# A streaming encoder trunk on one core: reordering the weight and adaLN transfers of the down projections, and writing y in eight transfers

## The chip, the cores and the metric

The kernel runs on one NeuronCore of a Trainium2 chip. The metric is the time of one execution on the device in microseconds (us), the median of several runs. The profile is one further execution, taken by the hardware profiler.

## The reference, cut to what matters

Two layers run over 544 tokens (512 of a prompt, 32 of a running stream), 1024 features wide. Each layer is a half-step SwiGLU FFN, a mixer (latent attention and retention heads), and a second half-step FFN. Each of the three is normalised before and after, and shifted, scaled and gated by vectors that come from a conditioning vector c.

```python
mods = (jax.nn.silu(c) @ ada_w[l] + ada_b[l]).reshape(c.shape[0], 3 * N_SUB, D_MODEL)
h = modulated_pre(x, norm_pre[l, 0], mods, 0)
x = gated_post(x, swiglu(h, ffn_w1[l, 0], ffn_w3[l, 0], ffn_w2[l, 0]), norm_post[l, 0], mods, 0, 0.5)
...
def swiglu(h, w1, w3, w2):
    return (jax.nn.silu(h @ w1) * (h @ w3)) @ w2
```

The last product of `swiglu`, with `w2` (2816 x 1024), is the down projection. There are four in the program: two FFNs in each of two layers. Beside it, the kernel computes the `mods` of the sub-layers that follow.

## The kernel before

All work is written by hand for each engine, with semaphores between them; the order of an engine's instructions is the order in the code. Activations are held feature-major: 128 partitions, eight feature tiles, 544 tokens.

**The chain of a weight chunk.** Every weight is float32 and is multiplied as a sum of a high and a low part. SyncE (SP) loads a chunk into one of two slots of `raw` (`load_chunk`, L356); ScalarE (ACT) rounds it to `w_hi` (`high` L968, `high_at` L975); GpSimd (POOL) subtracts, giving `w_lo` (`low`, L458); TensorE (PE) multiplies (`tile3`, L545 to L549). Each has two slots. SP loads chunk n once the low part of chunk n-2 is made (`lo_done`). ACT rounds chunk n once PE has finished chunk n-2 (`w_used`) and the chunk has landed.

**A down projection.** It has 16 chunks of 704 KB (11 weight tiles of 128x128 each), two for each of the eight output tiles. They are called c0 to c15 here; PE's work on one is 66 matmuls. ACT's order in it is: round c2 and c3, square and scale output tile 0; round c4 and c5, square and scale output tile 1; and so on. The scaling (L1068) needs `mul_post`, a column of `mods`, so the first of them waits for VectorE (DVE) to make it (`post_columns`, L1316).

**The ada tiles.** `ada_w` comes in tiles of 128x1024 (512 KB), in a ring of four slots (`ADA_RING`). DVE multiplies each with the two conditioning rows and sums (`ada_group`, L1292, two operations for each tile), four tiles to a group; after a group two additions put the result into `mods` (L1300). The first FFN of a layer (s = 0) does 48 tiles during its down projection, the second (s = 1) 24. `mul_post` is ready after the first two groups. SP may load tile t once tile t-4 is consumed (`ada_done`). The ring lies over `h_hi`, the input of the up projection, so its first four loads wait until PE has used the last chunk of the up projection.

**Order on SP.** Weight chunks and ada tiles go through the same instruction stream on SP, so a load stands behind the waits of all loads ahead of it. In `down`, each chunk load is followed by a share of tiles: none, four, four and four in the first four chunks at s = 0, later three after each chunk; at s = 1 none, four, two, two, later two after each, and none in the last four.

**The end of a down projection.** Before PE may sum the squares by token (`token_sums`, L562), it waits for all ada tiles of the phase (`ada_done`), since these sums use the PSUM banks where the conditioning rows lie. Then follow the root on ACT (L982), the reciprocal (L1326) and, for each feature tile m, `wide_v` (L1333) and the addition to `x` (L1337 on DVE, L484 on POOL for m = 1, 3, 5).

**The end of the program.** SP waits for all eight tiles of `x`, sends y out in one transfer (L444), and waits for it.

Of the kernel before, what the change touches and what calls it, by code (L numbers as in the profile page):

```python
# [24 lines left out]
P = 128  # L25
D = 1024
DEPTH = 2
# [7 lines left out]
KD = D // P  # L35
# [11 lines left out]
DN_T = FT // 2  # L47
UP_C = 2 * FT
DN_C = 2 * KD
# [11 lines left out]
MODS = 9 * KD  # L61
ADA_RING = 4
# [34 lines left out]
def streaming_trunk(nc, a, o):  # L97
    ctx = ExitStack()
    with ctx:
        def sb(name, shape, dt=F32):  # L100
            return ctx.enter_context(nc.sbuf_tensor(name, shape, dt))
# [22 lines left out]
        def signal(name, per_layer, before=0):  # L124
            return Signal(ctx.enter_context(nc.semaphore(name)), per_layer, before)


        x = sb("x", [P, KD, T])
# [118 lines left out]
        w_used = signal("w_used", CH, 2)  # L247

        ada_landed = [signal(f"ada_landed{i}", 16 * MODS // ADA_RING, 16 * 16 // ADA_RING) for i in range(ADA_RING)]
        ada_done = signal("ada_done", 2 * MODS, 2 * 16)  # L250
# [4 lines left out]
        x_new = [signal(f"x_new{i}", 12, 4) for i in range(2)]  # L255
# [78 lines left out]
        y_out = signal("y_out", 0)  # L334
# [12 lines left out]
        @block.sync  # L347
        def _(sp):
            def load_ada(tile, slot):
                sp.dma_start(ada_w[:, slot, :], a["ada"][bass.ds(tile, 1)].rearrange("a p n -> p (a n)"))\  # L350
                    .then_inc(ada_landed[slot].sem, 16)

            def load_chunk(l, c, slot, src, width):

                sp.wait_ge(lo_done.sem, lo_done.at(l, c - 1))
                sp.dma_start(raw[:, slot, 0:width], src.rearrange("a p n -> p (a n)"))\  # L356
                    .then_inc(landed[slot].sem, 16)

            sp.dma_start(c_all[:, :, :], a["c"].partition_broadcast(P)).then_inc(c_in.sem, 16)
            for t in range(ADA_RING):  # L360
                load_ada(t, t)
            sp.dma_start(ada_b[:, :], a["ada_b"]).then_inc(const_first.sem, 16)
            sp.dma_start(g_pre[:, :], a["g_pre"]).then_inc(const_first.sem, 16)
            for t in range(ADA_RING, 12):
                sp.wait_ge(ada_done.sem, 2 * (t - ADA_RING + 1))
                load_ada(t, t % ADA_RING)
            sp.dma_start(x[:, :, :], a["x"]).then_inc(x_in.sem, 16)
            for t in range(12, 16):
                sp.wait_ge(ada_done.sem, 2 * (t - ADA_RING + 1))
                load_ada(t, t % ADA_RING)  # L370
            consts = [(ident, "ident"), (half_ones, "half_ones"), (k_decay, "k_decay"), (k_decays, "k_decays"),
                      (cross, "cross"), (own_head, "own_head"), (state_decay, "state_decay"),
                      (g_post, "g_post"), (g_lat, "g_lat")]
            for t, n in consts:
                sp.dma_start(t[tuple([slice(None)] * len(t.shape))], a[n]).then_inc(const_in.sem, 16)

            def ffn(l, s):
                base = FFN_C[s]
                with sp.Fori(0, UP_C // 2) as i:
                    for k in range(2):  # L380
                        load_chunk(l, base + i * 2 + k, k, a["w_up"][bass.ds((l * 2 + s) * UP_C + i * 2 + k, 1)], KD * P)

                first, per = ((0, ADA_A // 4), (ADA_A, ADA_B // 3))[s]

                def down(i, first_time=False, ada=True):
                    for k in range(4):
                        load_chunk(l, base + UP_C + i * 4 + k, k % 2,
                                   a["w_dn"][bass.ds((l * 2 + s) * DN_C + i * 4 + k, 1)], DN_T * P)
                        if first_time:

                            tiles = (0, 0, ADA_RING, (per + ADA_RING) // 2, per)[k:k + 2]
                        else:
                            tiles = (k * per // 4, (k + 1) * per // 4)
                        for t in range(*tiles) if ada else ():
                            if not first_time or t >= ADA_RING:
                                sp.wait_ge(ada_done.sem, ada_done.at(l, 2 * first + 2 * per * i + 2 * (t - ADA_RING + 1)))
                            elif t == 0:

                                sp.wait_ge(w_used.sem, w_used.at(l, base + UP_C))
                            load_ada(l * MODS + 16 + first + i * per + t, t % ADA_RING)  # L400

                down(0, first_time=True)
                with sp.Fori(1, 4 - s) as i:
                    down(i)
                if s == 1:
                    down(3, ada=False)

            for l in range(DEPTH):
                ffn(l, 0)
                for c in range(MIX_C):  # L410
                    load_chunk(l, MIX_C0 + c, c % 2, a["w_mix"][bass.ds(l * MIX_C + c, 1)], KD * P)
                    if c == 1:

                        sp.wait_ge(w_used.sem, w_used.at(l, MIX_C0))
                        sp.dma_start(rope_tab[:, :, :], a["rope"]).then_inc(tables.sem, 16)
                        sp.dma_start(state_in[:, :, :], a["state"][bass.ds(l, 1)].rearrange("a p i v -> p (a i) v"))\
                            .then_inc(tables.sem, 16)
                    if c == Z_C + 1:

                        sp.wait_ge(w_used.sem, w_used.at(l, MIX_C0 + Z_C))  # L420
                        sp.dma_start(decay[:, :, :], a["decay"]).then_inc(decay_in.sem, 16)
                    if c == OUT_C0 + 1:
                        sp.wait_ge(kv_ready.sem, kv_ready.at(l, 1))
                        sp.dma_start(o["kv"][bass.ds(l, 1)].rearrange("a p n -> p (a n)"), kv[:, :]).then_inc(stored.sem, 16)
                        sp.wait_ge(rope.sem, rope.at(l, 3))
                        sp.dma_start(o["kpe"][bass.ds(l, 1)].rearrange("a p n -> p (a n)"), kpe[0:ROPE, :]).then_inc(stored.sem, 16)
                        sp.wait_ge(st_ev.sem, st_ev.at(l, 16))
                        sp.dma_start(o["state_p"][bass.ds(l, 1)].rearrange("a p i v -> p (a i) v"), state_p[:, :, :])\
                            .then_inc(stored.sem, 16)
                        sp.dma_start(o["state_s"][bass.ds(l, 1)].rearrange("a p i v -> p (a i) v"), state_in[:, :, :])\  # L430
                            .then_inc(stored.sem, 16)

                        sp.wait_ge(ro_mm.sem, ro_mm.at(l, 4))
                        sp.dma_start(cache_kv[:, 0:PAST], a["cache_kv"][bass.ds(l, 1)].rearrange("a p n -> p (a n)"))\
                            .then_inc(caches.sem, 16)
                        sp.dma_start(cache_pe[:, 0:PAST], a["cache_pe"][bass.ds(l, 1)].rearrange("a p n -> p (a n)"))\
                            .then_inc(caches.sem, 16)
                        sp.dma_start(cache_tok[:, :, :], a["cache_tok"][bass.ds(l, 1)].rearrange("a p b r -> p (a b) r"))\
                            .then_inc(caches.sem, 16)
                ffn(l, 1)  # L440

            for new in x_new:
                sp.wait_ge(new.sem, new.at(DEPTH, 0))
            sp.dma_start(o["y"], x[:, :, :]).then_inc(y_out.sem, 16)  # L444
            sp.wait_ge(y_out.sem, 16)
            sp.wait_ge(stored.sem, stored.at(DEPTH, 0))


# [1314 lines left out]
```

## Time and profile before

| | us |
|---|---|
| median of 3 runs | 2562.56 (2561.49 to 2564.19) |
| profiled execution, its own time | 2563.67 |
| its span, first to last instruction | 2561.9 |
| PE busy | 2387.9 (93%) |
| DVE busy | 1295.2 (51%) |
| ACT busy | 809.5 (32%) |
| POOL busy | 892.4 (35%) |
| mean granted TensorE clock | 0.977 of full speed |
| mean DMA rate | 106 GB/s |

The span is what the trace covers; 1.8 us of the execution's own time lie outside it. Busy shares are averages over stages: PE is nearly always busy, so what counts is what lies between its instructions, and what runs at the end when it has finished.

### The profile page before, as it was taken

How to read it: one execution, taken by the hardware profiler on the slowest of the kernel's cores; microseconds unless marked ns; L12 is line 12 of the kernel's file. 1: busy time of each engine (PE TensorE's matmuls, PEld its weight loads, DVE VectorE, ACT ScalarE, POOL GpSimd, SP SyncE). 2: the span in 40 equal slices, each digit the busy share in tenths (PEclk: the TensorE clock that was granted, in tenths of full speed). 3: DMA queues.
4: the chain of work that ended last, by engine and by line, in shares of the span. 5: the costliest groups of instructions: out<-in, count | busy, mean ns of one | idle time of the engine just before them, and what ended most of it. 6: DMA issues, size and time to landing. Idle time of an engine off the chain costs nothing.

```text
span 2561.9 us, 44088 instructions
## 1 busy us (share of the span) xinstructions
PE 2387.9 (93%) x17588; PEld 2247.4 (88%) x17588; DVE 1295.2 (51%) x2006; ACT 809.5 (32%) x1371; POOL 892.4 (35%) x384
## 2 busy tenths in 40 slices
PE   1999999999888999999999999999988899999997
PEld 1999999899456999999989999999964588999996
DVE  7333379774473243337243334986835515333561
ACT  2332222433233432323242223224323334322321
POOL 1334334443000543334443433444420034343343
PEclk9999999999899999999999999999989999999998
DMA  6222268323100222226312223761220011222451
GB/s 223 75 90 82 90 231 287 118 84 112 41 1 1 66 83 85 87 86 238 136 58 90 82 89 137 281 242 60 80 80 33 1 44 64 90 82 90 173 206 59
DMA packets 71509, 272.50 MB, mean 106 GB/s; under 512 B 8641, under 2 KB 10049, under 8 KB 70529
## 3 DMA queue, kind: packets, MB, share of 16 engines
q1 hardware_dynamic: 71424, 271.35, 30.8%
q8 instruction: 56, 0.92, 0.1%
q14 instruction: 29, 0.23, 0.0%
HBM read 267.87 MB, written 3.45 MB: 106 GB/s over the span
## 4 chain that ended last, share of the span: by engine, by line
PE 77%; DVE 11%; issue 6%; ACT 2%; DMA 1%; POOL 1%; DVEq 0%; SPq 0%; POOLq 0%; ACTq 0%
PE ps L545 22%; PE ps L549 22%; PE ps L546 21%; PE ps L859 2%; PE ps L903 2%; PE ps L555 1%; DVE ret_q L1443 1%; PE ps L855 1%; DVE ret_k L1443 1%; PE ps L593 1%; DVE wide_v L1333 1%; DVE wide_v L1292 1%; PE ps L769 1%; DVE x L1337 1%; DVE h_lo L1352 1%
## 5 line engine op out<-in xcount | busy, mean ns | idle before, releaser
L458 POOL TENSOR_TENSOR w_lo<-raw,w_hi 128x1024 fp32r<-128x1024 f32 (+1 forms) x304 | 789.6, 2597 | 1604.1 <-ACT w_hi L975 1295.8
L545 PE MATMUL ps<-h_hi,w_hi 128*128 128x274 f32 x3296 | 897.8, 290 | 4.8 <-DVE z_tmp L1412 4.8
L546 PE MATMUL ps<-h_lo,w_hi 128*128 128x274 f32 x3296 | 898.7, 290 | 0.0
L549 PE MATMUL ps<-h_hi,w_lo 128*128 128x274 f32 x3296 | 690.4, 291 | 0.0
L545 PEld LDWEIGHTS ps<-h_hi,w_hi 128*128 128x128 f32 x3296 | 626.5, 190 | 6.3 <-issue 6.2
L546 PEld LDWEIGHTS ps<-h_lo,w_hi 128*128 128x128 f32 x3296 | 620.8, 188 | 0.2
L975 ACT CAST w_hi<-raw 128x1024 fp32r<-128x1024 f32 (+1 forms) x236 | 268.3, 1137 | 876.1 <-PE ps L549 736.6
L549 PEld LDWEIGHTS ps<-h_hi,w_lo 128*128 128x128 f32 x3296 | 521.1, 188 | 0.0
L545 PE MATMUL ps<-u_hi,w_hi 128*128 128x272 f32 x1408 | 380.7, 289 | 13.1 <-POOL w_lo L458 13.1
L546 PE MATMUL ps<-u_lo,w_hi 128*128 128x272 f32 x1408 | 381.0, 289 | 0.0
L1292 DVE CUSTOM_DVE_ANT_0 wide_v<-ada_w,ps 128x1024 bf16<-128x1024 f32 x288 | 332.0, 1216 | 47.4 <-DMA ada_w<-in_ada 29.1
L1370 DVE TENSOR_TENSOR wide_v<-ps,wide_rinv 128x548 f32<-128x548 f32 x88 | 64.1, 729 | 451.6 <-PE ps L549 451.6
L549 PE MATMUL ps<-u_hi,w_lo 128*128 128x272 f32 x1408 | 291.0, 288 | 0.0
L545 PEld LDWEIGHTS ps<-u_hi,w_hi 128*128 128x128 f32 x1408 | 266.3, 189 | 14.9 <-POOL w_lo L458 14.9
L546 PEld LDWEIGHTS ps<-u_lo,w_hi 128*128 128x128 f32 x1408 | 265.7, 189 | 0.0
L1375 DVE SCALAR_TENSOR_TENSOR wide_v<-wide_v,wide_s 128x512 f32<-128x512 f32 (+1 forms) x176 | 194.5, 1143 | 110.2 <-ACT wide_s L1031 110.2
L549 PEld LDWEIGHTS ps<-u_hi,w_lo 128*128 128x128 f32 x1408 | 222.8, 189 | 0.0
L583 PE MATMUL ps<-h_hi,w_hi 128*128 128x274 f32 x192 | 64.5, 356 | 68.4 <-ACT h_hi L998 59.9
L968 ACT CAST w_hi<-raw 128x1024 fp32r<-128x1024 f32 x68 | 71.1, 1046 | 170.7 <-PE ps L549 113.6
L1034 ACT CAST u_hi<-wide_v 128x544 f32 (+1 forms) x88 | 56.9, 647 | 214.3 <-DVE wide_v L1375 214.3
L1326 DVE RECIPROCAL tok_inv<-tok_root 128x5 f32<-128x5 f32 x6 | 1.1, 190 | 218.0 <-ACT tok_root L982 218.0
L583 PEld LDWEIGHTS ps<-h_hi,w_hi 128*128 128x128 f32 x192 | 46.0, 239 | 72.7 <-issue 59.9
(228 smaller groups left out, 2565.7 us busy)
## 6 DMA issues: line engine op xcount, KB each, us to landing
raw<-in_w_up SPq DMA_DIRECT2D x176, 512.0 KB, 3.2
ada_w<-in_ada SPq DMA_DIRECT2D x160, 512.0 KB, 4.5
raw<-in_w_dn SPq DMA_DIRECT2D x64, 704.0 KB, 4.9
raw<-in_w_mix SPq DMA_DIRECT2D x64, 512.0 KB, 3.3
decay<-in_decay SPq DMA_DIRECT2D x2, 2048.0 KB, 8.2
x<-in_x SPq DMA_DIRECT2D x1, 2176.0 KB, 8.9
rope_tab<-in_rope SPq DMA_DIRECT2D x2, 1088.0 KB, 4.9
out_y<-x SPq DMA_DIRECT2D x1, 2176.0 KB, 7.3
```

The lines of the kernel that those rows point to most:

```text
L458: pool.tensor_tensor(w_lo[:, slot, 0:width], raw[:, slot, 0:width], w_hi[:, slot, 0:width].bitcast(F32), ALU.subtract).then_inc(lo_done.se ...
L545: pe.matmul(ps[:, bank + t, 0:half], wh, hi[:, n], start=start, stop=False)
L546: pe.matmul(ps[:, bank + t, 0:half], wh, lo[:, n], start=False, stop=False)
L549: last = pe.matmul(ps[:, bank + t, 0:half], wl, hi[:, n], start=False, stop=stop)
L583: pe.matmul(ps[:, 2 * w + t, 0:HW], w_hi[:, w, k * P:(k + 1) * P], h_hi[:, k, n], start=k == 0, stop=False)
L859: pe.matmul(ps[:, j, 0:w], q_pe[:, h // 4, q], own_keys[h % 4][:, 0:w], start=False, stop=True)\
L968: nc.scalar.copy(w_hi[:, slot, 0:width], raw[:, slot, 0:width]).then_inc(hi_done.sem, 1)
L975: nc.scalar.copy(w_hi[:, k, 0:width], raw[:, k, 0:width]).then_inc(hi_done.sem, 1)
L1034: nc.scalar.copy(u_hi[:, bass.ds(i * 2 + f, 1), :].rearrange("p a n -> p (a n)"), tmp_v[:, f, :]).then_inc(up_hi.sem, 1)
L1292: v_.tensor_tensor_reduce(junk[v], ada_w[:, t, :], c_row, 1.0, 0.0, ALU.mult, ALU.add, acc[:, v, t:t + 1]).then_inc(ada_done.sem, 1)
L1370: v_.tensor_tensor(halves(wide_v[:, f, :]), wide_pair(4 * f + 2), halves(wide_rinv[:, :]), ALU.mult)\
L1375: v_.scalar_tensor_tensor(out=wide_v[:, f, at], in0=wide_v[:, f, at], scalar=wide_v[:, f, T + 2 * v:T + 2 * v + 1], in1=wide_s[:, f, at], ...
```

## The change

In both FFNs, the loads of c2 and c3 now follow right behind the first four ada tiles, and the next ada tiles come after them. At s = 0 every later share of tiles stands three tiles further back (`ahead = 3`): the load of c4 is preceded by tiles up to 8 where it was 11, and the last three tiles of the phase follow after the last share. At s = 1 only the place of c3 changes. At the end, y goes out in eight transfers of 272 KB, each as soon as its tile of `x` is ready.

```diff
                 first, per = ((0, ADA_A // 4), (ADA_A, ADA_B // 3))[s]
-
-                def down(i, first_time=False, ada=True):
+                ahead = 3 if s == 0 else 0
+
+                def load_dn(i, k):
+                    load_chunk(l, base + UP_C + i * 4 + k, k % 2,
+                               a["w_dn"][bass.ds((l * 2 + s) * DN_C + i * 4 + k, 1)], DN_T * P)
+
+                def ada_tile(i, t):
+
+                    sp.wait_ge(ada_done.sem, ada_done.at(l, 2 * first + 2 * per * i + 2 * (t - ADA_RING + 1)))
+                    load_ada(l * MODS + 16 + first + i * per + t, t % ADA_RING)
+
+                def down(i, ada=True):
                     for k in range(4):
-                        load_chunk(l, base + UP_C + i * 4 + k, k % 2,
-                                   a["w_dn"][bass.ds((l * 2 + s) * DN_C + i * 4 + k, 1)], DN_T * P)
-                        if first_time:
-
-                            tiles = (0, 0, ADA_RING, (per + ADA_RING) // 2, per)[k:k + 2]
-                        else:
-                            tiles = (k * per // 4, (k + 1) * per // 4)
-                        for t in range(*tiles) if ada else ():
-                            if not first_time or t >= ADA_RING:
-                                sp.wait_ge(ada_done.sem, ada_done.at(l, 2 * first + 2 * per * i + 2 * (t - ADA_RING + 1)))
-                            elif t == 0:
-
-                                sp.wait_ge(w_used.sem, w_used.at(l, base + UP_C))
-                            load_ada(l * MODS + 16 + first + i * per + t, t % ADA_RING)
-
-                down(0, first_time=True)
+                        load_dn(i, k)
+                        for t in range(k * per // 4, (k + 1) * per // 4) if ada else ():
+                            ada_tile(i, t - ahead)
+
+                load_dn(0, 0)
+                load_dn(0, 1)
+                sp.wait_ge(w_used.sem, w_used.at(l, base + UP_C))
+                for t in range(ADA_RING):
+                    load_ada(l * MODS + 16 + first + t, t)
+                load_dn(0, 2)
+                load_dn(0, 3)
+                for t in range(ADA_RING, per - ahead):
+                    ada_tile(0, t)
                 with sp.Fori(1, 4 - s) as i:
                     down(i)
                 if s == 1:
                     down(3, ada=False)
+                for t in range(per - ahead, per) if s == 0 else ():
+                    ada_tile(3, t)
...
-            for new in x_new:
-                sp.wait_ge(new.sem, new.at(DEPTH, 0))
-            sp.dma_start(o["y"], x[:, :, :]).then_inc(y_out.sem, 16)
-            sp.wait_ge(y_out.sem, 16)
+            for m in range(KD):
+                sp.wait_ge(x_new[m % 2].sem, x_new[m % 2].at(DEPTH - 1, 2 * (KD // 2) + m // 2 + 1))
+                sp.dma_start(o["y"][:, m, :], x[:, m, :]).then_inc(y_out.sem, 16)
+            sp.wait_ge(y_out.sem, 16 * KD)
```

## Rows read from the trace of the kernel before

**Rows 1.** The page: shares of the chain that ended last, by engine.
```profile
PE 77%; DVE 11%; issue 6%; ACT 2%; DMA 1%; POOL 1%; DVEq 0%; SPq 0%; POOLq 0%; ACTq 0%
```
**Rows 2.** Waits of PE in down projections 1, 2, 3: total us, times, longest.
```profile
PE ps L545 <- POOL w_lo L458: 5.6, 4, 3.2
...
PE ps L545 <- POOL w_lo L458: 1.1, 1, 1.1
...
PE ps L545 <- POOL w_lo L458: 5.5, 2, 3.2
```
**Rows 3.** Timeline of SP, down projection 1: start, duration, engine, line, transfer, count.
```profile
334.28 0.49 SPq L356 DMA_DIRECT2D raw<-in_w_dn  x1
343.00 7.18 SPq L350 DMA_DIRECT2D ada_w<-in_ada  x4
350.23 0.43 SPq L356 DMA_DIRECT2D raw<-in_w_dn  x1
...
361.29 0.34 SPq L356 DMA_DIRECT2D raw<-in_w_dn  x1
```
**Rows 4.** Timeline of ACT, down projection 1; in brackets idle time before and its releaser.
```profile
332.49 1.37 ACT L975 CAST w_hi<-raw 128x1408 fp32r<-128x1408 f32 x1 [4.77 <-PE ps L549]
...
355.74 1.37 ACT L975 CAST w_hi<-raw 128x1408 fp32r<-128x1408 f32 x1 [11.10 <-DMA raw<-in_w_dn]
...
361.50 0.84 ACT L1068 ACTIVATE o_ffn<-ps,mul_post 128x272 f32<-128x272 f32 x2 [3.87 <-DVE mul_post L1316]
```
**Rows 5.** Timeline of POOL, down projection 1: the low part of c3.
```profile
357.19 3.17 POOL L458 TENSOR_TENSOR w_lo<-raw,w_hi 128x1408 fp32r<-128x1408 f32 x1 [9.25 <-ACT w_hi L975]
```
**Rows 6.** Windows of one chunk: us, busy PE, PEld, DVE, ACT, POOL, clock, DMA share, GB/s.
```profile
357.10:365.40 8.30, 5.14 (x29) 4.99 (x28) 7.61 (x19) 1.55 (x5) 3.17 (x1) 0.79 0.82 272
...
1193.30:1201.60 8.30, 7.19 (x57) 7.08 (x57) 7.28 (x15) 2.80 (x5) 5.72 (x3) 1.00 0.71 259
```
**Rows 7.** Timeline of ACT, down projections 2 (two rows) and 3 (the last).
```profile
1160.38 1.37 ACT L975 CAST w_hi<-raw 128x1408 fp32r<-128x1408 f32 x1 [4.76 <-PE ps L549]
...
1188.91 0.84 ACT L1068 ACTIVATE o_ffn<-ps,mul_post 128x272 f32<-128x272 f32 x2 [8.33 <-DVE mul_post L1316]
...
1580.08 1.37 ACT L975 CAST w_hi<-raw 128x1408 fp32r<-128x1408 f32 x1 [4.76 <-PE ps L549]
```
**Rows 8.** Timeline of PE: first token sums, ending down projections 1, 2 and 3.
```profile
472.73 1.17 PE L562 MATMUL ps<-ones,squares 128*128 128x1 f32 x10
...
1293.85 1.17 PE L562 MATMUL ps<-ones,squares 128*128 128x1 f32 x10
...
1719.69 1.17 PE L562 MATMUL ps<-ones,squares 128*128 128x1 f32 x10
```
**Rows 9.** Timeline of DVE: a pause, and the last ada tiles of projections 1 and 3.
```profile
433.79 2.56 DVE L1300 TENSOR_TENSOR mods<-acc,ada_b 128x4 f32 x2 [0.16 <-DVE acc L1292]
...
466.19 0.08 DVE L1292 DVE_READ_ACCUMULATOR2_ANT acc<- 128x1 f32 x1
...
1714.11 0.08 DVE L1292 DVE_READ_ACCUMULATOR2_ANT acc<- 128x1 f32 x1
```
**Rows 10.** DMA issues: transfer, count, KB each, median us from issue to landing.
```profile
ada_w<-in_ada SPq DMA_DIRECT2D x160, 512.0 KB, 4.5
raw<-in_w_dn SPq DMA_DIRECT2D x64, 704.0 KB, 4.9
...
out_y<-x SPq DMA_DIRECT2D x1, 2176.0 KB, 7.3
...
out_kv<-kv SPq DMA_DIRECT2D x2, 272.0 KB, 4.1
...
out_state_p<-state_p SPq DMA_DIRECT2D x2, 128.0 KB, 1.9
```
**Rows 11.** Windows inside the y transfer and before it; columns as in group 6.
```profile
2544.00:2554.00 10.00, 0.00 (x0) 0.00 (x0) 9.83 (x13) 0.00 (x0) 4.00 (x3) 0.55 0.00 0
...
2556.00:2558.00 2.00, 0.00 (x0) 0.00 (x0) 0.00 (x0) 0.00 (x0) 0.00 (x0) 0.50 1.00 418
```

## The prediction, made before the changed kernel was run

> **What bounds the kernel now.** I read the page first. The chain that ended last is PE for 77% [rows 1], so a change in the transfers can only gain where PE stands still, or after PE's last instruction. The waits of PE, asked for each down projection, show where it stands still: 5.6 us in four waits in the first, 1.1 us in the second, 5.5 us in the third [rows 2]; the fourth repeats the second (1.0 us). The releaser is the low part of a weight chunk, made by POOL, so the chain of that chunk is followed back.
>
> In projection 1, SP issues the load of c2 at 334.28, then four ada tiles from 343.00 to 350.2, and only then c3 at 350.23 [rows 3]. The tiles wait for DVE to free their slots, and c3 stands behind them in SP's stream although its own slot is long free. ACT is idle 11.1 us for it and rounds at 355.74 [rows 4]; POOL makes the low part from 357.19 to 360.4 [rows 5]; PE stands still for 3.2 us [rows 2]. The same happens to c4, behind four more tiles, at 361.29 [rows 3]. The windows show a second price: after the long wait the granted clock is 0.79 of full speed over a chunk's time, while after the 1.1 us wait of projection 2 it is 1.00 [rows 6]. So the 3.2 us wait is followed by a stretch at the lower level (1.2 GHz), and the short one is not.
>
> The whole price is best read from the length of a projection, from the rounding of c1 (released when PE begins) to the first token sums [rows 4, 7, 8]:
>
> - projection 1: 472.73 - 332.49 = 140.24 us
> - projection 2: 1293.85 - 1160.38 = 133.47 us
> - projection 3: 1719.69 - 1580.08 = 139.61 us
>
> All have the same 16 chunks. Those with 48 ada tiles lose 6.8 and 6.1 us against those with 24.
>
> **Part 1: c2 and c3 ahead of tiles 4 and on.** At s = 0, c3 can go out behind c2 once its slot is free, some 10 us sooner than 350.23, and lands long before PE asks for it. The 3.2 us wait and the slow clock behind it go. c4 now follows tile 8 instead of tile 11. DVE consumes a tile in about 2.3 us (the four issues spanning 7.18 us are three such steps plus the first issue [rows 3]), so c4 goes out about 3 x 2.4 = 7 us sooner, near 354, and lands by the median of 4.9 us [rows 10] near 359.
>
> Then something else is late: ACT. Before c4 it scales output tile 0, which needs `mul_post`. That comes at 361.50 - 332.49 = 29.0 us after the start in projection 1 and 28.5 us in projection 2 [rows 4, 7]. It depends only on DVE's eight tiles, which the change leaves alone. In projection 2 exactly this leaves PE 1.1 us short at c4 [rows 2]. So I take for projections 1 and 3 the length of 2 plus the 0.5 us by which `mul_post` comes later: 133.47 + 0.5 = 133.95 us.
>
> **Part 2: the next bound, DVE.** PE may not start its token sums before all 48 tiles are done. DVE's last one ends at 466.27 - 332.49 = 133.8 us in projection 1 and 1714.19 - 1580.08 = 134.1 us in projection 3 [rows 4, 7, 9]. Before, 6.4 and 5.5 us of slack hid this. Now it comes level with PE: 133.95 against 133.85, and 133.95 against 134.15 (each with 0.05 for the semaphore). The later of the two counts:
>
> - projection 1: 140.24 - 133.95 = 6.3 us gained
> - projection 3: 139.61 - 134.15 = 5.5 us gained
>
> Does the shift by three tiles make DVE later? A tile may be loaded when the tile four before it is done, and is wanted three tiles on, 3 x 2.3 + 1.1 (the additions between groups) = 8 us later; it lands in 4.5 us by the median [rows 10]. What could hold it is the chunk load now ahead of it, which waits for the low part of chunk n-2. For c5 that is some 6 us earlier than the slot of its next tile comes free, and some distance stays up to c15: PE's 12 chunks of 8.3 us, 1.6 for the c4 wait and 4.7 for rounding and low part of c13 give 106 us, while the slot of its next tile (42) comes free after 39 tiles, at about 108 us by the pace of DVE. So SP still waits for DVE and not for POOL; the shift costs nothing. If this cover went, each us would be paid in full, since DVE has no slack left. The other way, c16 (the first mixer chunk) now stands behind tiles up to 47 and lands about 128 us after the start; PE wants it only after the turn-over, over 10 us later.
>
> At s = 1 only c3 moves. PE did not wait for it, only for `mul_post` at c4, which stays: 0 us. The two clock stretches are in the lengths and are not counted again. The mixer's loads shift with the rest, since the same order on SP follows.
>
> **Part 3: y.** One transfer of 2176 KB lands 7.3 us after its issue [rows 10], at 418 GB/s in the middle [rows 11]. The eight tiles of `x` are made one after another in the 10 us before it, with DVE busy and no DMA [rows 11]. A piece of 272 KB takes 0.67 us at that rate, so seven are gone or nearly so when the last tile is ready, and SP needs under 0.5 us for each issue [rows 3]. Only the last piece counts. It is bounded by a write of 128 KB, 1.9 us, and one of 272 KB, 4.1 us, which shared the DMA engines with loads [rows 10]. Worked out from the big one: 7.3 less 5.3 us of moving is 2.0, plus 0.67, gives 2.6; I take 2.5. Gain 7.3 - 2.5 = 4.8 us (3.2 to 5.4).
>
> **The sum.** 6.3 + 5.5 + 4.8 = 16.6 us. The profiled execution's own time is 2563.67, its span 2561.9, so it stands 1.1 us above the median of the runs, 2562.56. From its own time the sum gives 2547.1; from the median, by which the result is judged, 2546.0. I predict 2546.0.
>
> A rule of the Trainium skill speaks against part 3. On the page "DMA: Bandwidth & Descriptors", section "Anatomy of one DMA", a transfer costs a fixed 2.0 us and its bytes at 436 GB/s. By that an estimate for the large one is 7.1 us, which the 7.3 us row bears out, and 2.6 us for a piece; the section "Bandwidth" advises transfers of 1 MiB or more.
>
> **The rivals.**
>
> *The eight pieces are not in flight together.* If each had to wait for the one before, they would take 8 x 2.6 = 21 us from about 2545, when the first tile is ready [rows 11], and end at 2566 instead of 2561.5: part 3 costs 4.5 us instead of giving 4.8, and the time is 2555.3. The advice of the named page on small transfers would bite in this case. Against it: SP issues three ada tiles 2.3 us apart, each landing in 4.5 us [rows 3, 10], so transfers overlap. Chance 3%.
>
> *DVE becomes the bound by more than a hair.* At three places in projection 1 the additions to `mods` took longer than their usual 0.3 us, up to 2.6 us [rows 9]. With no slack, one more of these in each projection costs 2 x 2.3 = 4.6 us: 2550.6. Chance 18%.
>
> *The c4 wait drops the clock.* If it grows from 1.6 to over 2 us in both, PE gets a slow stretch there, some 2 us each (140.24 - 133.47 less 5.6 - 1.1 of waits leaves 2.3 for the slow clock): 2550.4. Chance 10%.
>
> *The stall moves on.* c5 or c6 come late instead, by half of what is gained now (5.9 us): 2551.9. For it: the DMA share is already 0.82 there [rows 6]. Against: both go out over 3 us before they are wanted. Chance 7%.
>
> *DVE is starved* (the slower side). The chunk ahead of each three tiles holds them beyond the 8 us of cover. There are 13 such places in each of two projections; the sum is eaten when each costs 16.6 / 26 = 0.64 us, and at 1.3 us each the time is 2563 + 17 = 2580. This needs tiles landing in over 9 us against 4.5 [rows 10]. Chance 4%.
>
> **How the numbers follow.** Likeliest case, as summed: 58%, with 2543.5 to 2549 as its own range (y at its bounds, `mul_post` half a us either way, pauses on DVE smaller or larger). A measurement here tells 0.2%, about 5 us, from no change; so faster means below 2557.4, and all cases but starvation lie there; part of unforeseen ones may not. Faster 0.91, same 0.05, slower 0.04. The range of 8 in 10 takes in the DVE, clock and moved-stall cases: 2543.0 to 2552.5.
>
> **What would show it.** Right: c3 issued before 341 in projection 1; no wait of PE over 2 us in any down projection, one of 1 to 2 us at c4 in each; clock 1.00 in the chunk behind it; lengths of projections 1 and 3 near 134 us, 2 and 4 unchanged; the last ada tile and the token sums within 0.5 us of each other; last y piece landing 2 to 3 us after its issue. Wrong: idle DVE before L1292 with a DMA as releaser in projections 1 and 3; token sums released by DVE more than 1 us late; PE waits at c5 or later.

## The result and the profile after

The changed kernel takes 2556.37 us (median of 12 runs, 2551.33 to 2560.58), the kernel before, measured beside it, 2562.30 us (12 runs, 2559.77 to 2564.32). The ratio is 0.9976 with an interval of 0.9968 to 0.9985: 0.24% faster, a little more than the 0.2% that a measurement can tell from no change. The forecast was 2546.0 us with a range from 2543.0 to 2552.5, so 5.9 us came of 16.6, and the time lies above the range. The span of the profiled execution is 2555.6 us, 6.3 us less than the one before.

I look first at what the change was to do directly. The timeline of SP in down projection 1, after:

```profile
334.15 3.23 SPq L356 DMA_DIRECT2D raw<-in_w_dn  x2
342.88 11.10 SPq L350 DMA_DIRECT2D ada_w<-in_ada  x5
354.31 1.09 SPq L356 DMA_DIRECT2D raw<-in_w_dn  x1
```

Both c2 and c3 are out by 337.4, and c4 goes out at 354.31, 7.0 us sooner than in [rows 3]. And the DMA issues of the page:

```profile
out_y<-x SPq DMA_DIRECT2D x8, 272.0 KB, 2.1
```

A piece of y lands 2.1 us after its issue, against 7.3 for the whole [rows 10]. So the orders went where they were meant to go. Now the waits of PE in down projection 1, 2 and 3 (us in all, times, longest), after:

```profile
PE ps L571 <- DVE acc L1301: 1.8, 1, 1.8
...
PE ps L554 <- POOL w_lo L467: 1.6, 1, 1.6
...
PE ps L554 <- POOL w_lo L467: 1.1, 1, 1.1
...
PE ps L554 <- POOL w_lo L467: 4.1, 1, 4.1
...
PE ps L571 <- DVE acc L1301: 1.8, 1, 1.8
```

The 3.2 us waits for c3 [rows 2] are gone. What is new is a wait for DVE (`acc`, the ada tiles) at the end of projections 1 and 3, 1.8 us each, and a wait of 4.1 us at c4 in projection 3, where projection 1 has 1.6. Both end at work that DVE has not done yet.

Lengths, from the rounding of c1 (332.36 and 1576.03 in the ACT timeline after) to the first token sums:

| projection | before | forecast | after |
|---|---|---|---|
| 1 | 140.24 | 133.95 | 468.26 - 332.36 = 135.90 |
| 2 | 133.47 | 133.47 | 133.47 |
| 3 | 139.61 | 134.15 | 1717.20 - 1576.03 = 141.17 |
| 4 | 133.39 | 133.39 | 133.39 |

Projection 1 gained 4.3 us of 6.3. Projection 3 became 1.6 us longer where 5.5 us were to be gained. The timeline of PE at the two ends, after:

```profile
468.26 1.55 PE L571 MATMUL ps<-ones,squares 128*128 128x1 f32 x10 [1.80 <-DVE acc L1301]
469.67 2.27 PE L571 MATMUL ps<-ones,wide_s 128*128 128x1 f32 x10
...
476.42 0.60 PE L592 MATMUL ps<-h_hi,w_hi 128*128 128x274 f32 x1 [2.54 <-ACT h_hi L1007]
...
1717.20 1.25 PE L571 MATMUL ps<-ones,squares 128*128 128x1 f32 x10 [1.82 <-DVE acc L1301]
...
1725.06 0.59 PE L592 MATMUL ps<-h_hi,w_hi 128*128 128x274 f32 x1 [2.54 <-ACT h_hi L1007]
```

From the token sums to the first matmul of the mixer it takes 8.16 and 7.86 us. Before, it took 6.23 us behind projection 1 (from 472.73 [rows 8]) and 6.76 us behind projection 3 (from 1719.69 to 1726.45):

```profile
473.76 1.25 PE L562 MATMUL ps<-ones,wide_s 128*128 128x1 f32 x10
...
478.96 0.60 PE L583 MATMUL ps<-h_hi,w_hi 128*128 128x274 f32 x1 [2.54 <-ACT h_hi L998]
```

That is another 1.9 and 1.1 us lost.

The account of the two traces, span against span: 0.1 gained before projection 1; +4.3 in it; -1.9 in its turn-over; +1.6 in the mixer of the first layer; 0 in projection 2; -1.6 in projection 3; -1.1 in its turn-over; +0.1 up to projection 4; +4.8 from there to the end, where y is. Together 6.3 us. The 1.6 us of the mixer can't be put down to the change: in the trace of the kernel that has only the y part (below), whose loads are as before, the mixers of the two layers take 393.3 and 395.3 us from their first matmul to their token sums, where the trace of the kernel before has 395.2 and 393.5.

**Where DVE lost the time.** Its work is the same, 2006 instructions on both pages, but it is busy for 1307.6 us instead of 1295.2. Of the 12.4 us more, 8.3 are longer additions to `mods` in projections 1 and 3, and 4.1 are two operations behind them (`mul_pre`, below). Timeline of DVE in projection 3, after (the bracket gives idle time and its releaser):

```profile
1592.52 1.22 DVE L1301 CUSTOM_DVE_ANT_0 wide_v<-ada_w,ps 128x1024 bf16<-128x1024 f32 x1
...
1593.94 3.32 DVE L1309 TENSOR_TENSOR mods<-acc,ada_b 128x4 f32 x2 [0.20 <-DVE acc L1301]
1597.55 1.22 DVE L1301 CUSTOM_DVE_ANT_0 wide_v<-ada_w,ps 128x1024 bf16<-128x1024 f32 x1 [0.29 <-DVE mods L1309]
```

Two additions on 128x4 take 3.32 us. Elsewhere the same pair takes 0.28 or 0.29. Nothing stands in brackets that would explain it: a wait inside an instruction counts as its busy time. So I looked at what the other engines did in these 3.3 us, and found POOL:

```profile
1594.02 3.22 POOL L467 TENSOR_TENSOR w_lo<-raw,w_hi 128x1408 fp32r<-128x1408 f32 x1 [3.31 <-ACT w_hi L984]
```

POOL's subtraction ends at 1597.24 and the addition at 1597.26. In the kernel before, the pause of 433.79 [rows 9] meets POOL in the same way:

```profile
433.03 3.22 POOL L458 TENSOR_TENSOR w_lo<-raw,w_hi 128x1408 fp32r<-128x1408 f32 x1 [3.71 <-ACT w_hi L975]
```

It starts in the middle of that subtraction and ends with it, at 436.3. In all kernels of this study each addition over 0.4 us ends at most 0.03 us from the end of an instruction of POOL. Mostly that is a subtraction of weights; for the rest, which take at most 1.4 us, it is an operation on the squares (128x544, about 1.35 us). (The Trainium skill says so on the page "SBUF — State Buffer", section "SBUF: two separate sides": an operation of VectorE with two inputs in SBUF and one of GpSimd that reads SBUF take one port pair in turns, each for its whole instruction. The trace agrees: 0.15 us became up to 3.2.)

A pair costs 0.3 us or up to 3.3, by where it meets POOL. Counting what the additions took over their usual 0.16 us, from their rows in the timelines: projection 1 went from 5.4 to 6.5 us, projection 3 from 4.9 to 12.2 us, with four pauses of about 3 us each. Not all of this lies ahead of the last ada tile: the last pair of a projection stands behind it, and before the change that pair held 1.6 and 0.6 us. Ahead of the last tile the pauses were 3.8 and 4.3 us and became 6.3 and 11.9.

The time from the last reduction of a group to the first of the next shows what DVE lost by them, since a pause takes the place of a part of the idle time there. The eleven such steps of a projection took 28.5 us in projection 1 and 28.4 in projection 3 before, and 30.5 and 35.3 after: 2.0 and 6.9 us more. That is the whole delay of the last tile. It ends at 1717.05 - 1576.03 = 141.0 us after the start in projection 3, against 134.1 before [rows 9], and at 135.75 against 133.8 in projection 1.

The pauses also differ where the order of the loads is the same. With only the y part of the change the last tile ends 136.3 us after the start in projection 1 and 133.1 in projection 3, with 7.2 and 3.5 us of pauses ahead of it. So the 2.0 us of projection 1 are no more than what two traces of one order differ by; the 6.9 us of projection 3 are more.

The first of the four pauses in projection 3 lies before `mul_post`, which so comes 31.5 us after the start instead of 29.0. ACT stands at L1077 for it:

```profile
1576.03 1.37 ACT L984 CAST w_hi<-raw 128x1408 fp32r<-128x1408 f32 x1 [4.77 <-PE ps L558]
...
1607.56 0.84 ACT L1077 ACTIVATE o_ffn<-ps,mul_post 128x272 f32<-128x272 f32 x2 [13.09 <-DVE mul_post L1325]
1608.46 1.37 ACT L984 CAST w_hi<-raw 128x1408 fp32r<-128x1408 f32 x1
```

This makes c4 4.1 us late, and PE then works at a lower granted clock for a while. Windows of 8 us behind the c4 wait, projection 1 and projection 3, after (columns as in [rows 6]; the clock is third from the end):

```profile
365.00:373.00 8.00, 6.42 (x52) 6.20 (x51) 7.65 (x15) 2.80 (x5) 6.45 (x3) 1.00 0.87 305
...
1612.00:1620.00 8.00, 6.88 (x32) 6.88 (x33) 7.82 (x11) 2.80 (x5) 3.82 (x2) 0.57 0.89 294
```

After a wait of 1.6 us the granted clock is 1.00, after 4.1 us it is 0.57, nearer to the lower level (1.2 GHz) than to the upper. The turn-over pays for the clock once more. PE has just stood for 1.8 us; behind projection 1 its token sums take 1.55 and 2.27 us, where 1.17 and 1.25 were usual. Windows of 2 us from the first token sums on, after (two rows) and before:

```profile
468.30:470.30 2.00, 2.00 (x13) 2.00 (x14) 1.97 (x3) 0.00 (x0) 2.00 (x2) 0.68 0.95 400
470.30:472.30 2.00, 1.64 (x8) 1.55 (x8) 1.03 (x7) 0.32 (x2) 0.60 (x1) 0.50 0.98 377
...
472.70:474.70 2.00, 2.00 (x21) 2.00 (x19) 0.00 (x0) 1.56 (x2) 0.14 (x1) 1.00 0.41 74
```

The granted clock is 0.68 and then 0.50, the lower level, where it was 1.00. This is all of the 1.9 and 1.1 us: 1.4 and 1.1 in the token sums, and 0.5 in the four small matmuls behind them after projection 1. DVE's `mul_pre`, which also reads two tiles in SBUF, meets POOL there too:

```profile
468.72 2.28 DVE L1318 SCALAR_TENSOR_TENSOR mul_pre<-mods,g_pre 128x8 f32<-128x8 f32 x2
```

But DVE is idle again, for 0.97 us, before the reciprocal that PE waits for, so this pause costs nothing.

### The profile page after: what moved, and what is told of

Same layout as the page of the kernel before. It is cut to its first block, busy times and chain, and to the rows that moved or that the text cites. A ratio compares the mean times of both kernels' runs of the same rounds, so it can differ in the third digit from the quotient of the medians.

```text
span 2555.6 us, 44094 instructions
## 1 busy us (share of the span) xinstructions
PE 2387.6 (93%) x17588; PEld 2246.8 (88%) x17588; DVE 1307.6 (51%) x2006; ACT 808.9 (32%) x1371; POOL 892.0 (35%) x384
## 4 chain that ended last, share of the span: by engine, by line
PE 70%; DVE 13%; issue 10%; ACT 2%; DMA 2%; DVEq 0%; POOL 0%; SPq 0%; ACTq 0%
PE ps L558 19%; PE ps L554 19%; PE ps L555 19%; DVE wide_v L1301 2%; PE ps L868 2%; PE ps L912 2%; PE ps L564 1%; DVE ret_q L1452 1%; PE ps L864 1%; DVE ret_k L1452 1%; DMA ada_w<-in_ada 1%; PE ps L602 1%; DVE wide_v L1342 1%; PE ps L778 1%; DVE x L1346 1%
```

## The experiments

My theory after the result: the orders work as forecast, and the gain is lost because DVE, now level with PE, stands still where its additions meet POOL's long subtraction. Rivals: the gains of the weights and of y get in each other's way; the shift by three tiles hurts; what holds DVE is its transfers.

**The two halves.** One kernel with only the y part of the change, one with only the order of the weights.

```diff
 # y only: the loads as before; weights only: y in one transfer as before
-            sp.dma_start(o["y"], x[:, :, :]).then_inc(y_out.sem, 16)
+            for m in range(KD):
...
+                sp.dma_start(o["y"][:, m, :], x[:, m, :]).then_inc(y_out.sem, 16)
```

> The kernel before with part 3 alone: y in eight transfers, the weights' order as before. After the change the last piece landed 2.1 us after its issue against 7.3 us for the whole. My theory: the whole of it is kept, 5.2 us, a ratio near 0.998. Rival (the gain of the changed kernel came from the order of the weights): 1 us or less.

> The changed kernel with y in one transfer again. Theory: the reordering of the weights gives 1 us on average (-1 to 3 us), since what PE gains at c3 and c4 (about 6 us in projection 1) is given back at the end, where it waits for DVE. Rival: it gives 5 us or more and the profiled execution of the changed kernel was an unlucky one.

Measured: y alone 2557.07 us (11 runs, 2554.71 to 2559.23), ratio 0.9978, interval 0.9969 to 0.9987. The weights alone 2560.45 us (11 runs, 2556.57 to 2565.11), ratio 0.9992, interval 0.9983 to 1.0001. So y brings 5.6 us with an interval of some 2 us either way, in line with the 5.2 us by which the landing is shorter. The order of the weights brings 2.1 us, not told from nothing, as its interval takes in 1. Both are as expected. The halves add up to the whole, within their intervals: the first rival falls, and what is missing is missing in the weights.

**The additions taken out.** DVE's reduction can take the bias as its initial value and write into `mods` itself. This kernel has the ada loops of DVE written out too, so a second kernel writes the loops out and keeps the additions. The additions taken out with the loops kept was not tried.

```diff
 # loops written out (the four ada loops of DVE in ffn)
-                with dve.Fori(0, 4) as i:
+                for i in range(4):
...
 # and, in the other kernel alone, the bias as the initial value
-                        v_.tensor_tensor_reduce(junk[v], ada_w[:, t, :], c_row, 1.0, 0.0, ALU.mult,
-                                                ALU.add, acc[:, v, t:t + 1]).then_inc(ada_done.sem, 1)
+                        v_.tensor_tensor_reduce(junk[v], ada_w[:, t, :], c_row, 1.0, bias, ALU.mult,
+                                                ALU.add, mods[:, v, n0 + t:n0 + t + 1]).then_inc(ada_done.sem, 1)
...
```

Not shown: the two additions go, and what waited for them (`columns`) waits for `ada_done`.

> Control for the next kernel: the changed kernel with DVE's ada loops written out, the additions to mods kept. Theory: nothing but the instruction stream of DVE changes, so within 2 us of the changed kernel, and long additions (1.3 to 3.3 us where 0.2 us is usual) still appear while GpSimd subtracts. Rival (the long additions are waits for instructions at the ends of loops): they vanish here.

> The changed kernel with the additions to mods gone: the bias is the initial value of the reduction, which writes into mods (loops written out as in the control). All outputs as before. Theory: the small additions have two inputs in SBUF and stand still while GpSimd's subtraction runs; without them DVE needs 48 x 2.3 = 110 us for the tiles, done by 119 us after the start, mul_post comes about 27 us after the start instead of 29, the c4 wait goes, and projections 1 and 3 take 132.5 us, 2 and 4 about the same: 2 x 5 to 7 us less than the changed kernel in 1 and 3 (and no slow clock at the turn-over), 2 x 1 us in 2 and 4: 2541 to 2546 us in all. Rival (the additions are not what is late; the tiles are, since they are shifted): DVE then waits for DMA before L1301 in projections 1 and 3 and the time stays above 2550 us.

Measured: loops written out 2541.48 us (4 runs, 2537.57 to 2542.24), ratio 0.9917, interval 0.9902 to 0.9932. Additions out as well: 2541.9 us (5 runs, 2537.13 to 2543.38), ratio 0.9915, interval 0.9901 to 0.9928. The two tie. The expectation for the first failed: it had the long additions right and the time wrong by 15 us. The second came in its range, but not by its own sum: DVE's last tile ends 125.5 and 126.4 us after the start, not 119. A reduction took 1.28 us there instead of 1.22, and DVE waited 1.3 and 2.2 us for transfers. Its rival had such waits and a time above 2550 us; the waits are there but small, and the time is far below, so it falls. The timeline of DVE, first the changed kernel with its loops:

```profile
390.24 1.22 DVE L1301 CUSTOM_DVE_ANT_0 wide_v<-ada_w,ps 128x1024 bf16<-128x1024 f32 x1
391.38 0.08 DVE L1301 DVE_READ_ACCUMULATOR2_ANT acc<- 128x1 f32 x1
391.63 0.29 DVE L1309 TENSOR_TENSOR mods<-acc,ada_b 128x4 f32 x2 [0.16 <-DVE acc L1301]
392.51 1.22 DVE L1301 CUSTOM_DVE_ANT_0 wide_v<-ada_w,ps 128x1024 bf16<-128x1024 f32 x1 [0.59 <-DVE mods L1309]
```

and the one with the loops written out:

```profile
398.19 1.22 DVE L1301 CUSTOM_DVE_ANT_0 wide_v<-ada_w,ps 128x1024 bf16<-128x1024 f32 x1
399.33 0.08 DVE L1301 DVE_READ_ACCUMULATOR2_ANT acc<- 128x1 f32 x1
399.45 0.23 DVE L1309 TENSOR_TENSOR mods<-acc,ada_b 128x4 f32<-128x4 f32 x2
399.81 1.22 DVE L1301 CUSTOM_DVE_ANT_0 wide_v<-ada_w,ps 128x1024 bf16<-128x1024 f32 x1
...
409.07 3.07 DVE L1309 TENSOR_TENSOR mods<-acc,ada_b 128x4 f32<-128x4 f32 x2
```

From the last reduction of a group to the first of the next it takes 392.51 - 390.24 = 2.27 us with the loop and 399.81 - 398.19 = 1.62 us without. The difference of 0.65 us comes up to eleven times in a projection of 48 tiles, at most 7.2 us of DVE's time; a long pause hides a part of it. Pauses of 3.07 us are still there, 6.9 and 6.5 us in all in projections 1 and 3. Yet DVE now has slack, its last tile ending 130.3 us after the start in both, and PE waits for it neither at c4 nor at the end: the lengths are 132.49 and 132.50. A pause costs nothing while DVE has slack. The changed kernel has none, by the forecast's own account, and each pause is paid.

**The written out loops without the change.**

> The kernel before with DVE's ada loops written out, nothing else. In the changed kernel that gave 15 us. Theory: in the kernel before DVE is not what PE waits for at the end, so writing out gives less there: the c3 wait stays (SP still holds c3 behind four tiles), only mul_post and the c4 wait gain; 2556 to 2560 us, 3 to 6 us faster. The order and y together are then worth 15 to 18 us on top of it, the 16.6 us of the prediction. Rival (the unrolled loops save something that has nothing to do with the order of transfers): it gives 15 us here too, 2548 us.

Measured 2559.87 us (11 runs, 2555.88 to 2563.09), ratio 0.9986, interval 0.9976 to 0.9996. Lighter loops alone are worth some 3 us, and the time lies in the expected range. In the trace 1.5 us of this come in projections 2 and 4, which are 132.49 and 132.84 us long instead of 133.47 and 133.39. With them the change is worth 2559.87 - 2541.48 = 18.4 us. The two intervals together leave more than 4 us either way, so this is about the 16.6 forecast. So DVE is not a second, independent loss: it decides what the change is worth.

**The pauses made short, and nothing else.** POOL's subtraction of a down chunk in four instructions of 352 columns. DVE's code and loops stay as they are. This experiment touches the suspected cause and leaves DVE's own instructions alone.

```diff
-                pool.tensor_tensor(w_lo[:, slot, 0:width], raw[:, slot, 0:width], w_hi[:, slot, 0:width].bitcast(F32),
-                                   ALU.subtract).then_inc(lo_done.sem, 1)
+                n = 4 if width == DN_T * P else 1
+                for part in range(n):
+                    r = slice(part * width // n, (part + 1) * width // n)
+                    last = pool.tensor_tensor(w_lo[:, slot, r], raw[:, slot, r], w_hi[:, slot, r].bitcast(F32),
+                                              ALU.subtract)
+                last.then_inc(lo_done.sem, 1)
```

> The changed kernel, loops kept, but GpSimd's subtraction of a down-projection chunk (3.2 us) made in four instructions of 352 columns. Theory (the small additions of DVE stand still until the GpSimd instruction that runs has ended): no addition takes over 1.1 us, the last ada tile of projections 1 and 3 is done at most 132 us after the start instead of 136 and 141, PE does not wait for it, and the time is 2545 to 2549 us, the time of the prediction. Rival (the long additions come with the ends of loops or with DMA): they keep their 1.3 to 3.3 us and the time stays within 2 us of 2556.

> The kernel before with the same split. Theory: shorter stalls of DVE there too, but PE does not wait for DVE at the end; only mul_post can come earlier. 2559 to 2562 us, 0 to 3 us faster. Rival as for the split in the changed kernel: nothing moves.

Measured with the change: 2544.22 us (5 runs, 2542.46 to 2546.43), ratio 0.9932, interval 0.9918 to 0.9946. Without it: 2561.35 us (10 runs, 2559.2 to 2563.15), ratio 0.9998, interval 0.9989 to 1.0007. Cutting an instruction of an engine that never was the bound is worth nothing before the change and 12.2 us after it. The timelines of DVE and POOL where they meet, changed kernel with the cut:

```profile
1684.85 0.92 DVE L1313 TENSOR_TENSOR mods<-acc,ada_b 128x4 f32 x2 [0.18 <-DVE acc L1305]
1685.95 1.22 DVE L1305 CUSTOM_DVE_ANT_0 wide_v<-ada_w,ps 128x1024 bf16<-128x1024 f32 x1 [0.19 <-DVE mods L1313]
...
1684.73 3.67 POOL L470 TENSOR_TENSOR w_lo<-raw,w_hi 128x352 fp32r<-128x352 f32 x4 [3.29 <-ACT w_hi L988]
```

The four parts take 3.67 us together, some 0.4 more than the whole. The first addition ends with the first of the four parts, at 1685.69, with three still to come: the pair takes 0.92 us instead of 3.3. No addition in the down projections takes more than 0.93 us, and they cost 3.5 us in each of projections 1 and 3 instead of 6.5 and 12.2. DVE's last tile ends at 131.3 us in both. The waits of PE in projection 1 and 3:

```profile
PE ps L558 <- POOL w_lo L470: 1.3, 1, 1.3
...
PE ps L558 <- POOL w_lo L470: 1.4, 1, 1.4
```

No wait for `acc`, and only the short one at c4 that was forecast. The lengths are 133.70 and 133.71 us, where 133.95 and 134.15 were predicted, and the time is 1.8 us under the forecast (and 0.8 under the range that was expected of this run).

**The shift by three tiles.** The change with `ahead` at 0: the first chunks as in the change, tiles up to 11 ahead of c4 again.

```diff
-                ahead = 3 if s == 0 else 0
+                ahead = 0
...
-                for t in range(per - ahead, per) if s == 0 else ():
+                for t in ():
```

> The changed kernel with ahead = 0: only c2 and c3 go ahead of tiles 4 and on, later tiles as before. Theory: the c3 wait goes (3.6 us with its slow clock), c4 again stands behind tile 11 and comes late by about what it did, 3 to 5 us, so most of the gain in projections 1 and 3 moves to c4; 2556 to 2560 us. Rival (the shift by three is what makes DVE late at the end): the waits for DVE at the token sums vanish and the time is below 2553.

> The changed kernel with the loops written out and ahead = 0. It asks what the shift by three tiles is worth once DVE has slack. Theory: c4 stands behind tile 11 and lands too late, PE waits 3 to 6 us for it in projections 1 and 3 with a slow clock behind: 2549 to 2556 us. Rival (the shift is worth nothing, only c3 counted): 2541 us.

Measured: 2561.4 us (10 runs, 2556.98 to 2563.99), ratio 0.9994, interval 0.9985 to 1.0003. With the loops written out 2556.11 us (5 runs, 2549.32 to 2556.78), ratio 0.9968, interval 0.9955 to 0.9981. SP and the waits of PE in projection 1 with `ahead` at 0:

```profile
343.26 17.95 SPq L350 DMA_DIRECT2D ada_w<-in_ada  x8
361.55 0.34 SPq L356 DMA_DIRECT2D raw<-in_w_dn  x1
```

```profile
PE ps L554 <- POOL w_lo L467: 6.2, 2, 6.0
```

Without the shift the stall of c3 moves on whole to c4, issued at 361.55, as late as before. The shift is worth 5.0 us in the changed kernel (2561.4 against 2556.37) and 14.6 us where DVE has slack (2556.11 against 2541.48). Both times lie a little above what was expected (2560 and 2556 us at most); in projection 3 PE waits 8.9 us at c4 without the shift and with the loops kept, since a pause delays `mul_post` there again. The second rival, that the shift hurts, falls: the time is not below 2553. With the loops kept, DVE's last tile does come sooner without the shift, at 133.9 and 136.9 us after the start, with fewer pauses ahead of it. With them written out it comes at 129.7 us without and 130.3 with the shift, so the shift itself costs DVE next to nothing. The third falls too: in projections 1 and 3 no reduction of DVE waits for a transfer in the trace of the changed kernel, and each tile has landed at least 0.7 us before its first reduction.

**Both cures together.**

> The changed kernel with both: DVE's ada loops written out and the subtraction in four instructions. Theory: either alone takes DVE off the path (2541.5 and 2544.2 us), so the two don't add: 2539 to 2542 us. Rival (each has a saving of its own): 2529 us.

Measured 2541.64 us (5 runs, 2539.56 to 2543.22), ratio 0.992, interval 0.9907 to 0.9934, the same as each kernel with the loops written out. Once DVE has slack, shorter pauses bring no more. Three versions are level at about 2541.5 us, 15 us under the changed kernel and 21 under the one before. The smallest edit of the three is the loops written out.

## Why the prediction was wrong, step by step

- **c3, and c4 sooner (part 1): right.** c3 was out before 341, its wait and the slow clock behind it are gone, and c4 went out 7.0 us sooner, where about 7 was said.
- **`mul_post` then limits c4 (part 1): right in the mechanism.** The wait at c4 is 1.6 us in projection 1 and 4.1 in projection 3. The step "It depends only on DVE's eight tiles, which the change leaves alone" is true of the work and not of its duration: in projection 3 a pause of 3.2 us fell into these eight tiles.
- **s = 1 unchanged: right,** 133.47 and 133.39 us to the hundredth.
- **DVE's last tile (part 2): the step that failed.** "DVE's last one ends at ... 133.8 us in projection 1 and ... 134.1 us in projection 3. ... Now it comes level with PE" takes DVE's ends over from the trace before as if they were fixed. They hold 3.8 and 4.3 us of pauses whose number and length hang on where DVE meets POOL, and they are one trace's: with the same order of loads and only y changed they were 136.3 and 133.1. After the change they were 135.75 and 141.0. The step from there to PE's token sums was put at 0.05 us and measured 0.15. Of the 16.6 us forecast, 2.0 and 7.0 were lost in the lengths of projections 1 and 3. Another 1.9 and 1.1 were lost behind their ends, at the lower clock after PE's wait for DVE, for which the sum had no term. That is 12.0 us in the traces; 1.6 in the mixer and smaller terms gave 1.8 back.
- **"The shift costs nothing" (part 2): right** as far as the transfers go, and the shift is needed.
- **y (part 3): right,** 5.2 us at the landing where 4.8 was said. The pieces overlap: one goes out at 2545.94 and lands 2.35 us later, the next goes out at 2546.66. The last lands 2.03 us after its issue. The sum that the prediction takes from the page "DMA: Bandwidth & Descriptors" of the Trainium skill, section "Anatomy of one DMA", is given there for transfers that GpSimd issues; y goes out from SP. It makes 2.6 us for a piece, where 2.1 was measured. The advice to make transfers large did not decide here, since only the last piece stands behind the last tile.
- **The rival "DVE becomes the bound by more than a hair" was what happened,** with the right place, the additions to `mods`. It was priced at one more pause in each projection, 4.6 us in all, because the cause wasn't known. It cost 9.0 us in the lengths and 3.0 behind them. "The c4 wait drops the clock" came with it in projection 3. The two were priced as if each came alone, while one pause sets off both.

The forecast holds for a kernel in which DVE's pauses are short: with the cut subtraction the whole change, y included, is worth 2561.35 - 2544.22 = 17.1 us against 16.6. The two intervals leave some 4 us either way, so that they agree this closely is in part luck.

**What stays open.** Why the meetings with POOL were so many more after the change in projection 3, four of 3 us in one projection, isn't shown. The weights-only kernel has four over 1 us there as well, 10.4 us of pauses ahead of the last tile. DVE's group of additions comes every 10.3 us and POOL's subtraction about every 8.3, so a small shift of one against the other can change which of them meet, but this is only argued. Why a turn of DVE's loop costs 0.65 us isn't shown either, nor what makes a mixer take 393 us in one trace and 395 in another.

## What to carry to other kernels

- When a change takes away the wait in front of the engine that sets the end, measure how much slack the next engine has, and what part of its time is variable. A number read from a trace in which that engine had slack may hold pauses that were free there, and another trace with the same order of loads may hold others: here the end that one trace gave as 133.8 us came at 136.3 in another.
- An instruction whose duration differs twentyfold between equal shapes is waiting inside. No list of waits shows it. Compare its end with the ends of the other engines' instructions; if they match, cut the long instruction of the other engine, take the short one out, or give the engine slack.
- The price of such an edit can't be read from the kernel as it is: cutting POOL's instruction brought nothing before the change of order and 12 us after it.

## What the runs showed of the hardware

- VectorE's TENSOR_TENSOR on 128x4 with both inputs in SBUF took 0.15 us, or up to 3.2 us while a GpSimd TENSOR_TENSOR that reads SBUF ran, and then ended within 0.03 us of it. A pair of SCALAR_TENSOR_TENSOR on 128x8 took 2.28 us in the same way, where such a pair usually takes 0.23. The reduction of 128x1024 with one input in PSUM took 1.22 us with POOL busy or not.
- GpSimd's subtraction of 128x1408 took 3.22 us in one instruction and about 3.65 us in four.
- A turn of VectorE's loop over a group of tiles cost 0.65 us more than the same instructions written out.
- Eight transfers of 272 KB behind one another, issued as their tiles came ready, landed 2.1 us after their issue each, by the median.
